# One core, two blocks: loads, bias steps, crossing products and scaling reordered

## What is computed

```python
# first block
mod = silu(c) @ w_ada + b_ada                 # 6 x 1024; sh1, sc1 are its first third
h = rms(x, norm1_g) * (1 + sc1) + sh1
proj = h @ w_in                               # then MLA heads and differential attention
bias = rel_bias[bucket(pos_k - pos_q)]        # added to the scores of the differential attention,
s = where(chunk_k <= chunk_q, s + bias, -inf) # and 16 experts follow the attention
# second block, in each of 2 layers
a = b_gate * causal_conv3(c_gate * xa)                       # short convolution
xbc = silu(causal_conv4(xbc) + b); xs, B, C = split(xbc)     # SSD, 16 heads in 4 groups
acs = cumsum(-exp(a_log) * dt)
y[h] = (C @ B.T [group] * exp(acs_l - acs_s) * (s <= l)) @ (xs * dt)[h]
# then retention, stick-breaking attention, four gated branches and a feed-forward part
```

## Time and profile before

| | us |
|---|---|
| median of 3 runs | 2410.71 (2407.94 to 2413.88) |
| profiled execution, its own time | 2406.68 |
| its span | 2404.9 |
| PE busy | 2273.7 (95%) |
| PE weight loads busy | 2118.0 (88%) |
| DVE busy | 1617.3 (67%) |
| ACT busy | 1183.0 (49%) |

### The profile page before, as it was taken

The page is one execution under the profiler, slowest core; times in us unless marked ns, Lnnn a source line. Parts: engine busy times, 40 slices in busy tenths (PEclk is TensorE's granted clock), DMA queues, the critical chain, the costliest instruction groups (busy, mean ns, idle before and its releaser), DMA issues.

```text
span 2404.9 us, 37105 instructions
## 1 busy us (share of the span) xinstructions
PE 2273.7 (95%) x15890; PEld 2118.0 (88%) x15890; DVE 1617.3 (67%) x2050; ACT 1183.0 (49%) x1403; POOL 0.2 (0%) x4
## 2 busy tenths in 40 slices
PE   6999899999899899999998999899899999998997
PEld 5787788888798789999888999799789999998997
DVE  7987799999695457546556664695458445656764
ACT  1534477777453344534754444353344535845442
POOL 0000000000000000000000000000000000000000
PEclk8999899999999899999999999899899999999999
DMA  7454399999454234434334354354234444343552
GB/s 295 144 189 145 133 372 373 369 369 376 177 178 158 88 105 161 170 126 158 123 106 158 141 177 174 116 182 140 106 108 173 159 157 142 120 143 141 180 182 95
DMA packets 62325, 427.45 MB, mean 178 GB/s; under 512 B 7632, under 2 KB 9936, under 8 KB 11728
## 3 DMA queue, kind: packets, MB, share of 16 engines
q1 hardware_dynamic: 62160, 425.06, 48.6%
HBM read 423.99 MB, written 1.05 MB: 177 GB/s over the span
## 4 chain that ended last, share of the span: by engine, by line
PE 85%; DVE 9%; ACT 3%; issue 2%; DMA 0%; SPq 0%; ACTq 0%; DVEq 0%
PE banks L1790 59%; PE banks L1808 9%; PE quad L1808 5%; ACT area_y_rounded L653 2%; DVE area_y L2265 2%; PE single L1524 1%; DVE slot_rounded L982 1%; PE quad L461 1%; PE single L573 1%; PE quad L524 1%; PE quad L560 1%; PE quad L548 1%; PE quad L508 1%; DVE slot_rounded L2295 1%; PE quad L563 1%
## 5 line engine op out<-in xcount | busy, mean ns | idle before, releaser
L1790 PE MATMUL banks<-spare_rounded,slot_rounded 128*128 128x272 f32 (+1 forms) x2176 | 628.0, 289 | 0.0
L1790 PE MATMUL banks<-spare_rounded,area_y_rounded 128*128 128x272 f32 (+1 forms) x1504 | 443.9, 295 | 12.8 <-DVE hn_rounded L971 12.8
L1790 PE MATMUL banks<-area_x_rounded,slot_rounded 128*128 128x272 f32 (+1 forms) x1568 | 446.7, 285 | 0.0
L1790 PE MATMUL banks<-hn_rounded,area_y_rounded 128*128 128x272 f32 (+1 forms) x1504 | 436.2, 290 | 0.0
L1790 PEld LDWEIGHTS banks<-spare_rounded,slot_rounded 128*128 128x128 f32 x2176 | 417.2, 192 | 0.0
L982 DVE TENSOR_TENSOR slot_rounded<-slot,area_y_rounded 128x2048 fp32r<-128x2048 f32 x118 | 269.8, 2290 | 211.0 <-ACT area_y_rounded L653 210.5
L1790 PEld LDWEIGHTS banks<-spare_rounded,area_y_rounded 128*128 128x128 f32 x1504 | 290.6, 193 | 16.8 <-DVE hn_rounded L971 13.6
L1790 PEld LDWEIGHTS banks<-area_x_rounded,slot_rounded 128*128 128x128 f32 x1568 | 296.4, 189 | 0.0
L1790 PEld LDWEIGHTS banks<-hn_rounded,area_y_rounded 128*128 128x128 f32 x1504 | 290.4, 193 | 0.1
L653 ACT ACTIVATE area_y_rounded<-slot 128x2048 fp32r<-128x2048 f32 x118 | 223.9, 1906 | 48.4 <-PE banks L1790 48.4
L982 DVE TENSOR_TENSOR slot_rounded<-slot,area_x_rounded 128x2048 fp32r<-128x2048 f32 x52 | 119.0, 2292 | 93.1 <-ACT area_x_rounded L653 93.0
(11 more groups left out here) (545 smaller groups left out, 5239.8 us busy)
## 6 DMA issues: line engine op xcount, KB each, us to landing
slot<-in_units_second SPq DMA_DIRECT2D x236, 1024.0 KB, 4.8
slot<-in_units_moe SPq DMA_DIRECT2D x100, 1024.0 KB, 4.9
slot<-in_units_first SPq DMA_DIRECT2D x32, 1024.0 KB, 4.9
spare<-in_units_moe SPq DMA_DIRECT2D x20, 1024.0 KB, 5.0
spare<-in_units_first SPq DMA_DIRECT2D x6, 1024.0 KB, 5.1
slot<-in_units_second SPq DMA_DIRECT2D x8, 768.0 KB, 4.2
slot<-in_units_first SPq DMA_DIRECT2D x2, 576.0 KB, 3.7
h<-in_x SPq DMA_DIRECT2D x1, 1024.0 KB, 8.3
```

The costliest lines, as they stand in the source:

```text
L1790: ins = nc.tensor.matmul(out, weights[w], x[a], start=start and i == 0, stop=stop and i == 2, **kw)
```

## The change

**Loads and first block.** SP loads `x` ahead of unit 0, with a semaphore of its own, and the first constants behind unit 0; the rest of the constants goes out behind the load of the fourth unit of `w_in`. The frequencies of the rotation move to the parameters. PE sums the squares of `x` ahead of the eight units of `w_ada`. DVE makes distances, steps (three instructions in place of 30) and angles before it waits for the constants, and the first bias step takes the place of the copy of the chunk mask, which one addition over four heads brings in later. Two bias steps stand ahead of the modulation, one behind each of the first two pairs, `weights_low(0)` in the third and `weights_low(1)` in the fourth; ACT rounds units 0, 1, 2 behind pairs 1, 2, 3. Of the steps that go from the start, two come ahead of `read_ada(8)` and one more each in items 2 and 5 of the attention.

**Layers.** The crossing products stand behind group 5 of the convolution; DVE masks them behind tile 2. The turns stand behind groups 12, 16 and 19. `scale_inner` stands ahead of `seen`. Two spreads stand ahead of the heads and each head spreads the one two further on; ACT clips two heads ahead, with the clip behind the exponential. The spreads and clips use all 272 columns and 128 rows.

```diff
@@ second_tensor
-    for g in plan.conv[:12]:
+    for g in plan.conv[:6]:
+        group(g)
+    pe.wait_ge(s.xbc.sem, s.xbc.at(L, 16))
+    for g in range(SSD_GROUPS):
+        ...
+        tick(ins, s.crossed)
+    for g in plan.conv[6:12]:
         group(g)
...
             if b:
                 pe.wait_ge(s.xdt.sem, s.xdt.at(L, 2 * b + half - 1))
+            else:
+                pe.wait_ge(s.masked.sem, s.masked.at(L, 3 + half))
...
-    turned_behind = {plan.conv[12]: 0, plan.conv[15]: 1, plan.conv[18]: 2}
+    turned_behind = {plan.conv[12]: 0, plan.conv[16]: 1, plan.conv[19]: 2}
...
-    for g in range(SSD_GROUPS):
-        if g >= 2:
-            pe.wait_ge(s.xdt.sem, s.xdt.at(L, g + 3))
...
     spread(0)
+    spread(1)
     for h in range(SSD_HEADS):
-        if h + 1 < SSD_HEADS:
-            spread(h + 1)
+        if h + 2 < SSD_HEADS:
+            spread(h + 2)
@@ second_scalar
     clip(0)
+    clip(1)
     for h in range(SSD_HEADS):
-        if h + 1 < SSD_HEADS:
-            clip(h + 1)
...
+        if h + 2 < SSD_HEADS:
+            act.wait_ge(s.exped.sem, s.exped.at(L, h + 1))
+            clip(h + 2)
@@ second_vector
         tick(tt(w.ya[:, t, :], y[:, Q], bank(gb), ALU.mult), s.dve_free)
+        if t == 2:
+            for g in range(SSD_GROUPS):
+                v.wait_ge(s.crossed.sem, s.crossed.at(L, g + 1))
+                tick(tt(m.work[:, g, 0:PACKED], m.quad[:, 512 * g:512 * g + PACKED], m.causal, ALU.mult), s.masked)
+        if t in (4, 5, 6):
+            scale_inner(t - 4)
         seen(gc, gx, gb)
...
-        if t in (4, 5, 6):
-            scale_inner(t - 4)
@@ first_sync
+    sp.dma_start(x_to, x_of).then_inc(m.loaded_x.sem, 16)
     load(0)
-    for to, of in m.early_loads:
-        sp.dma_start(to, of).then_inc(m.loaded_early.sem, 16)
+    sp.dma_start(const_to, const_of).then_inc(m.loaded_early.sem, 16)
...
@@ first_tensor
+    pe.wait_ge(s.x_squared.sem, 1)
+    for k in range(KT):
+        ins = nc.tensor.matmul(m.quad[:, 1536:1536 + SEQ], m.ones[:, :], m.sq1[:, k, :], ...)
+    tick(ins, s.x_stat)
+    for u in ADA_EARLY:
         ada_rows(u)
@@ first_scalar
-    weights_high(0)
     for pair in range(KT // 2):
         ...
+        for n in ((), (0,), (1,), (2,))[pair]:
+            weights_high(n)
@@ first_vector
-    bias_steps(4)
...
     link(tt(m.h1, m.x, m.root1.unsqueeze(1).to_broadcast([128, KT, SEQ]), ALU.mult))
-    bias_steps(4)
     for pair in range(KT // 2):
-        if pair == 2:
-            weights_low(0)
...
+        if pair < 2:
+            bias_steps(1)
+        elif pair == 2:
+            weights_low(0)
         v.wait_ge(s.h1_high.sem, pair + 1)
         tick(tt(m.h1_low[:, both, :], ...), s.h1_low)
+        if pair == 3:
+            weights_low(1)
...
-    bias_steps(1)
+    bias_steps(3)
     read_ada(8)
...
         if i < 7:
-            bias_steps(1)
+            bias_steps(2 if i in (2, 5) else 1)
```

More of the change, by code:

```diff
@@ L397, in second_tensor @@
     tick(ins, s.dt_ready)
-    for g in plan.conv[:12]:
+    for g in plan.conv[:6]:
+        group(g)
+    pe.wait_ge(s.xbc.sem, s.xbc.at(L, 16))
+    for g in range(SSD_GROUPS):
+        out = strips(m.quad, 512 * g, q0)
+        for b in range(3):
+            t0, n = KEYS[b]
+            ins = nc.tensor.matmul(out[b], m.xc[:, KT + g, t0:t0 + n], m.xc[:, KT + SSD_GROUPS + g, max(t0, q0):T], start=True, stop=True)
+        tick(ins, s.crossed)
+    for g in plan.conv[6:12]:
         group(g)
@@ L723, in clip @@
         act.wait_ge(s.spread.sem, s.spread.at(L, h + 1))
-        out, at = strips(m.work[:, 4 + h % 2, :], 0, q0), 512 * (h % 2)
+        bank = m.quad[:, 512 * (h % 2):512 * (h % 2) + T]
+        out = [m.work[:, 6 + h % 2, at:at + cols] for b, (at, cols) in sorted(STRIP.items())]
         for b, (t0, n) in enumerate(KEYS):
-            tick(f(out[b], m.quad[0:n, at + max(t0, q0):at + T], ACT.Relu, scale=-1.0, bias=m.acs_col[0:n, b, h:h + 1]), s.clipped if b == 2 else s.act_step)
+            tick(f(out[b], bank[:, t0:], ACT.Relu, scale=-1.0, bias=m.acs_col[:, b, h:h + 1]), s.clipped if b == 2 else s.act_step)
     act.wait_ge(s.columns.sem, s.columns.at(L, 1))
     clip(0)
+    clip(1)
     for h in range(SSD_HEADS):
-        if h + 1 < SSD_HEADS:
-            clip(h + 1)
         act.wait_ge(s.clipped.sem, s.clipped.at(L, h + 1))
@@ L735, in second_scalar @@
             act.wait_ge(s.weighted.sem, s.weighted.at(L, h - 1))
-        tick(f(m.work[:, 6 + h % 2, 0:PACKED], m.work[:, 4 + h % 2, 0:PACKED], ACT.Exp, scale=-1.0), s.exped)
+        else:
+            act.wait_ge(s.dve_free.sem, s.dve_free.at(L, plan.conv[20 + 3 * h].freed))
+        tick(f(m.work[:, 4 + h % 2, 0:PACKED], m.work[:, 6 + h % 2, 0:PACKED], ACT.Exp, scale=-1.0), s.exped)
+        if h + 2 < SSD_HEADS:
+            act.wait_ge(s.exped.sem, s.exped.at(L, h + 1))
+            clip(h + 2)
         if h == 2:
@@ L1536, in first_tensor @@
     pe.wait_ge(s.silu_c_ready.sem, 1)
-    for n, u in enumerate(ADA_EARLY):
-        ada_rows(u)
[L1539 to L1543, removed]
+    pe.wait_ge(s.x_squared.sem, 1)
+    for k in range(KT):
+        ins = nc.tensor.matmul(m.quad[:, 1536:1536 + SEQ], m.ones[:, :], m.sq1[:, k, :], start=(k == 0), stop=(k == KT - 1))
+    tick(ins, s.x_stat)
+    for u in ADA_EARLY:
+        ada_rows(u)
     def low_ready(unit):
@@ L2226, in first_vector @@
     link(copy(m.pos[:, :], m.pos_int[:, :]))
[L2227 to L2231, removed]
+    for q, (a, n) in enumerate(((0, 128), (128, 256))):
+        tick(ts(m.rel[:, a:a + n], m.pos[:, 2:2 + n], m.pos[:, q:q + 1], None, ALU.subtract), s.dve1_step)
+    for at, of, before, n in ((0, 0, 1, 15), (15, 17, 0, 1), (16, 18, 17, 14)):
+        tick(tt(m.steps[:, 4 * at:4 * (at + n)], p1("rel_bias", 4 * of, 4 * n), p1("rel_bias", 4 * before, 4 * n), ALU.subtract), s.dve1_step)
     for b in range(2):
-        tick(ts(m.angle[:, b, :], m.inv_freq, m.pos[:, b:b + 1], None, ALU.mult), s.dve1_step)
+        tick(ts(m.angle[:, b, :], p1("inv_freq", 0, MLA_ROPE // 2), m.pos[:, b:b + 1], None, ALU.mult), s.dve1_step)
     settle()
@@ L2350, in rope @@
         settle()
-    weights_low(1)
     weights_low(2)
@@ L2693, in program @@
         m.work = Area(work).cut(10, WORK)
-        m.conv, m.ctanh, m.cc, m.ztanh = (m.work[:, i:j, 0:T] for i, j in ((4, 7), (8, 10), (2, 4), (0, 2)))
+        m.conv, m.ctanh, m.cc, m.ztanh = (m.work[:, i:j, 0:T] for i, j in ((4, 7), (8, 10), (8, 10), (0, 2)))
         m.dt_arg, m.dt_abs = m.work[0:16, 7, 0:T], m.work[0:16, 7, T:2 * T]
```

81 lines of the change are left out of this document (41 added, 40 removed).

## The result

| | before | after |
|---|---|---|
| median of the runs, us | 2410.86 (2407.94 to 2413.88, 4 runs) | 2369.38 (2367.77 to 2370.14, 4 runs) |
| ratio | | 0.9829, 95% interval 0.9815 to 0.9844 |
| profiled execution, us | 2406.68, span 2404.9 | 2368.9, span 2367.1 |
| mean granted clock of TensorE | 0.971 | 0.978 |

The change makes the kernel 41.5 us faster; 48.8 were forecast, and 2362 for the median. The time lies within the range given and 7.4 us above the number.

What follows compares the result with a forecast made beforehand. PE's own split products bound most of the span, so time comes only from PE's waits. First block 15.8 - 4.4 = 11.4 plus layers 37.4 gave 48.8 us off, median 2362; own range 2353 to 2372, with three rivals 2350 to 2386.

Steps and rivals of the forecast that it cites:

- Start, 15.8 earlier: First block, start: the second subtraction behind the last pair ends at 51.8 instead of 67.6 us, and all 15.8 arrives.
- What comes back, 4.4: First block, attention: four bias steps moved behind the start cost 0.7, 1.2 and 2.5, together 4.4 us; bounds 0 and 10.0.
- the fourth step: Attention, item 5: the bias step behind `read_ada` has no cover before PE's next turn and costs 2.5 us.
- a fallen clock behind the gap in the layers: Rival, chance 0.15: the clock falls at the new gap ahead of the first head, 2.9 us a layer, 2368.
- Layers, 18.9 each: Each layer: waits gone 13.7, slow clock behind them 7.5, less a new stall of 2.3; two layers make 37.4 us.
- the new stall: End of each layer's convolution: PE's third spread waits for clip 0 behind ACT's copy, 2.3 us; bounds 0 and 5.2.
- Heads, nothing: Heads' loop: two-ahead spreads change nothing; the 7.1 us in twelve waits of the mixing product stay; bounds 0 and 7.1 gained.
- Sum: Whole kernel: 11.4 us from the first block plus 37.4 from two layers, 48.8 in all; median 2362.
- stalls move in the convolution: Rival, chance 0.10: PE waits for a delayed subtraction instead of scaling; half of a layer's gain stays, 2381.
- does nothing: Rival, chance 0.03: the heads' edit or whole change does nothing; all waits replaced by others of the same length gives 2410.
- slower: Rival, chance 0.03: in the heads ACT runs a head late, each head serialises 2.3 us, 32 heads make 75 us, 2437.
- Start gains half: Rival, chance 0.10: `x` lands later or four bias steps cost their full 10.0 us; price 5.6 to 8, 2369.

Runs made afterwards that it cites:

- layers only: The first block of the kernel before with the layers of the changed kernel: median 2378.75 us, ratio to before 0.985 to 0.9883.
- The halves: Two kernels, each the changed kernel with either its layers or its first block taken from before: medians 2401.62 and 2378.75 us.
- subtraction behind: The changed kernel with VectorE's subtraction for head h-1 moved from ahead of head h's multiplication to behind it: median 2362.39 us.
- scaling behind: The changed kernel with the scaling of the turned inner parts put back after the subtractions: median 2390.88 us.
- late copy: The changed kernel with ScalarE's last convolution copy after exponential 0 and VectorE's subtraction of it after multiplication 0: median 2364.39 us.

## Why the prediction was nearly right, step by step

*Start, 15.8 earlier.* Right, a little less. The seventh unit starts 98.04 - 82.64 = 15.4 earlier; turned rows come at 110.4 in the mean of twelve profiles with the new start and at 125.2 in two with the old, 14.8. The sum of the squares, now PE's first long piece, took 6.45, 0.9 more than the 5.57 of the first piece before, from which the prediction had taken it. PE's slack at the seventh unit was taken for 1.9 and the wait was 2.5, "about 1" was forecast; behind it PE's 48 products took 7.46. In "layers only", with the old start, they took 7.43, so this seems to cost nothing new: before's profile, with 5.88, is the only one of the fourteen under 7.3.

*What comes back, 4.4.* Wrong in size: the attention takes 107.6 for 100.3, so 7.3, where 3.7 of the 4.4 were forecast. The failed step is the price of the fourth step: "no cover is left before PE's next turn: 2.5". The wait was near the forecast (3.1, of which the edit removes 2.5), but the clock fell behind it, and the edit that moves the step away returns 5.6. I had priced a fallen clock behind the gap in the layers as a rival and not here. The 0.7 for the two steps ahead of `read_ada(8)` doesn't show in the start's rows, where the spread is larger.

*Layers, 18.9 each.* The waits went as forecast (13.7 a layer), and so did the new stall (2.4 for 2.3). 16.9 came; most of what lacks is the slow clock behind the new gap, 4.73 - 3.2 = 1.5 a layer, of which the forecast took none and a rival 2.9. That rival was half right in its mechanism. Its time, 2368, lies nearer to the measured 2369.4 than the forecast 2362 does, but by luck: the other half of the difference lay in the attention.

The Trainium skill ("TensorE: Matmul & The Clock Gate", "HAM oscillation") describes a loop whose work is shorter than its waits for data, and which pays for the slow clock in every round. Its waits are of about 3 to 5 us, longer than the 2.4 here, so by itself it did not give the rival's 2368. The granted clock of 0.79 over the gap and the group behind it in after agrees that a wait is paid for again; 1.00 over the same gap and group in another kernel, below, shows that it is not each time.

*Which edit does it.* The prediction listed the turns' waits as gone by scaling and place together; the place was worth nothing beside the scaling. The prediction also gave the crossings 3.3 less 2.3 and a share of the slow clock; they brought nothing that the layer's time shows.

*Heads, nothing.* Right for the loop: 7.0 in twelve waits for 7.1, period 9.8 as before.

*Sum.* 7.5 for 11.4 in the first block (14.8 - 7.3), 33.8 for 37.4 in the layers: 41.3, and 41.5 were measured. The halves run alone gave 9.7 and 32.6 by the medians, so how the 7.4 us that lack divide between the two is known to about 2 us only.

The rivals "stalls move in the convolution", "does nothing" and "slower" didn't come: PE never waited for L992 there, and ACT was never a head late. "Start gains half" came in part, by the second of its two ways: `x` landed on time, but 7.3 came back of the 10.0 that it allowed for, and it had priced 5.6 to 8 where some 3.6 were lost; and they were lost to the clock, not to further steps.

## What to carry to other kernels

An instruction placed behind another on an in-order engine inherits that one's wait, not just its duration: a move of three lines was worth 7.0 us of lead where the instruction passed took 2.2. Price a wait of TensorE of 2 to 3 us at about twice its length, since the products behind it ran at a lower granted clock in most places here: 2.5 us of wait cost 5.6 in the attention, 4.4 cost 9.7 to 10.0 in a layer's turns, 2.4 cost 3.9 ahead of most first heads. When several edits remove the same waits, undo each alone, and several together, before giving any of them credit, and make each alone in the old kernel too; and read a profile's luck off the stretches that the change doesn't touch, before subtracting two profiles.

## What the hardware showed that I had not expected

The same wait can cost differently. Windows over the gap ahead of the first head and the group behind it, first of after, then of the kernel with the subtraction behind:

```profile
800.40:808.40 8.00, 5.58 (x29) 5.07 (x29) 5.95 (x6) 6.30 (x12) 0.00 (x0) 0.79 0.36 131
```
```profile
804.00:811.00 7.00, 4.58 (x33) 4.07 (x32) 6.71 (x8) 5.89 (x11) 0.00 (x0) 1.00 0.41 150
```

In both PE stands 2.42 us, with the same work before it. The first then takes 4.73 us for its group of 24 products, the second 3.21. In layer 1 both take about the same (4.55 and 4.56). The cost is the rule and the 3.21 the exception: of the seven profiles with this gap in layer 0, five take 4.73 or 4.74, "scaling behind", with two more waits ahead of it, 5.74, and only this one 3.21; in layer 1 six take 4.52 to 4.57 and "scaling behind" 5.42. Behind the gap of 0.95 that "late copy" leaves, the group takes 3.21 and 3.03. What spared the one group stays open, and no run here was made for it. In the same way the seventh unit's products took 5.88 in one profile with the old start and 7.43 in the other.

The prediction named a drain behind the table load that the trace of before doesn't show: rows 9 have the load alone, which ends at 827.92, and the exponential starts at 827.94 in that trace. After's timeline of ACT doesn't show the drain either: the exponential of head 0 starts 0.01 us behind the end of its table load.

```profile
804.07 1.28 ACT L743 ACT_TABLE_LOAD   x1
805.36 0.56 ACT L743 ACTIVATE work<-work 128x432 f32<-128x432 f32 x1
```
